# Three edits in one kernel: a fused bias-and-maximum pass, an earlier signal, and a fetch order

## What is computed

```python
# sparse attention, for a block of 128 queries (528 keys: 16 meta tokens and 512 tokens)
_, sel = lax.top_k(score, topk)                       # 128 keys for each query
logits = jnp.einsum('bqhc,bqkc->bqhk', qf, kv_sel).astype(jnp.float32) * scale
logits = jnp.where(valid[:, :, None, :], logits, -1e30)
p = jax.nn.softmax(logits, axis=-1)
...
# experts: every token goes to 2 of 32
hid = jax.nn.silu(xe @ w1[e]) * (xe @ w3[e])          # w1, w3: 1024 x 512
return hid @ w2[e]                                    # w2: 512 x 1024
```

## Time and profile before

| | before |
|---|---|
| median of 3 runs | 2671.62 us (2663.79 to 2676.19) |
| the profiled execution | 2671.74 us, its span 2669.9 us |
| busy: TensorE, VectorE, ScalarE, GpSimd | 91%, 61%, 33%, 33% of the span |
| sparse attention | about 300 to 514 us |
| experts | about 645 to 1123 us |

### The profile page before, as it was taken

How to read it: one execution, slowest core, us unless ns; L and a number is a source line. 1 busy time by engine, 2 the same in 40 slices (tenths; PEclk the granted TensorE clock), 3 DMA queues, 4 the chain that set the end, 5 groups by cost and what they waited for, 6 DMA issues and landing times.

```text
span 2669.9 us, 32591 instructions
## 1 busy us (share of the span) xinstructions
PE 2418.1 (91%) x12845; PEld 1821.7 (68%) x12845; DVE 1623.2 (61%) x3273; ACT 868.5 (33%) x1619; POOL 882.5 (33%) x714
## 2 busy tenths in 40 slices
PE   9999888997888878789899967699999999999999
PEld 7756555675545444377675556588888888888887
DVE  5357567443100100054536999789988888898887
ACT  3135333431000000043422248633343333333333
POOL 0013211001110010000001169586666666566660
PEclk9999878997999998979999978899999999999999
DMA  4344110245999999641123006799999999999994
GB/s 186 124 174 181 52 44 32 98 189 232 411 426 426 426 426 425 265 171 67 41 86 150 25 20 241 249 409 398 367 399 392 388 388 391 358 394 397 407 394 144
DMA packets 137549, 693.66 MB, mean 260 GB/s; under 512 B 18364, under 2 KB 36836, under 8 KB 103600
## 3 DMA queue, kind: packets, MB, share of 16 engines
q1 hardware_dynamic: 76656, 479.68, 45.1%
q0 software_dynamic: 60736, 211.85, 20.4%
HBM read 659.52 MB, written 38.81 MB: 262 GB/s over the span
## 4 chain that ended last, share of the span: by engine, by line
PE 69%; DVE 17%; DMA 8%; ACT 4%; issue 2%; SPq 0%; DVEq 0%; ACTq 0%; POOLq 0%
PE psum L3422 13%; PE psum L3388 11%; DMA arena<-w 7%; PE psum L1706 6%; PE psum L2752 4%; PE psum L2217 4%; PE psum L466 4%; PE psum L982 4%; PE psum L1713 3%; DVE arena L3569 3%; DVE rounded L3519 2%; PE psum L3394 2%; PE psum L3392 2%; PE psum L1285 2%; PE psum L1300 2%
## 5 line engine op out<-in xcount | busy, mean ns | idle before, releaser
L3422 PEld LDWEIGHTS psum<-rounded,rounded 128*128 128x128 f32 x2880 | 429.7, 188 | 25.8 <-ACT rounded L3455 10.1
L3422 PE MATMUL psum<-rounded,rounded 128*128 128x320 f32 x2880 | 443.9, 310 | 0.3
L3388 PE MATMUL psum<-rounded,rounded 128*128 128x512 f32 x1536 | 399.3, 396 | 6.7 <-DVE rounded L3533 6.7
L3335 POOL DMA_INDIRECT arena<-u_rows,arena x192 | 295.6, 1540 | 152.4 <-DVE arena L3574 48.8
L3335 POOL DMA_INDIRECT arena<-v_rows,arena x192 | 286.1, 1490 | 168.8 <-DVE arena L3580 73.3
L3388 PEld LDWEIGHTS psum<-rounded,rounded 128*128 128x128 f32 x1536 | 284.3, 189 | 82.3 <-issue 19.6
L1706 PE MATMUL psum<-arena 128*64 128x256 f32 x2048 | 256.6, 414 | 62.5 <-issue 47.9
L3519 DVE TENSOR_TENSOR rounded<-arena,rounded 128x1024 fp32r<-128x1024 f32 x248 | 302.3, 1219 | 8.1 <-ACT rounded L3455 8.1
L1706 PEld LDWEIGHTS psum<-arena 128*64 128x64 f32 x2048 | 179.1, 150 | 151.7 <-issue 103.5
L1817 DVE COPY arena<-psum 128x256 f32<-128x256 f32 x32 | 13.6, 424 | 419.9 <-PE psum L1758 419.9
L3455 ACT ACTIVATE rounded<-arena 128x1024 fp32r<-128x1024 f32 x248 | 247.7, 1045 | 0.1
(11 more groups left out here) (473 smaller groups left out, 3762.1 us busy)
## 6 DMA issues: line engine op xcount, KB each, us to landing
arena<-w SPq DMA_DIRECT2D x96, 2048.0 KB, 27.8
arena<-uv SPq DMA_DIRECT2D x124, 1024.0 KB
arena<-wada SPq DMA_DIRECT2D x12, 2048.0 KB
arena<-gd SPq DMA_DIRECT2D x30, 640.0 KB
arena<-wp SPq DMA_DIRECT2D x8, 2048.0 KB
gd<-arena SPq DMA_DIRECT2D x11, 1024.0 KB, 11.3
arena<-win SPq DMA_DIRECT2D x4, 2048.0 KB
arena<-wq SPq DMA_DIRECT2D x4, 2048.0 KB
```

What stands on the lines that cost most here:

```text
L3335: po.indirect_dma_start(out=ROWS_OF[i % len(ROWS_OF)], out_offset=None, in_=src, in_offset=bass.IndirectOffsetOnAxis(ap=column.bitcast(U32 ...
L3388: ins = pe.matmul(PS[:, 2 * n + half, :], gg[:, z, 128 * n:128 * n + 128], v[:, y, 512 * half:512 * half + 512], x == 0 and i == 0, x == 1 ...
L3422: ins = pe.matmul(PS[:, 7, 0:DT], w[:, y, k, :], hv[:, z, :], k == 0 and i == 0, k == 7 and i == 2)
```

## The change

Three edits. (1) In the sparse attention one VectorE instruction forms `-(logits + bias)`, writes it to `PB`, and gives its row minimum, which is the negated row maximum of the sum, to `MX`; the separate maximum is gone, and ScalarE takes exp(-PB + MX). The signal `max` is gone with it, ScalarE waits for `logits`. (2) The up products of w1 and of w3 each wait for their own matrix only and signal apart, as `w1` and `h`; the SiLU waits for `w1`. (3) SP issues the fetches in the order w1(e), w3(e), w2(e - 1), in which TensorE uses them, and the fetch to the place of a w1 waits for the signal `w1`.

```diff
@@ sparse_ac
-                    ac.wait_ge(*D.dv["max", n, g, h])
-                    ac.activation(PB[:, h, 0:nk], PB[:, h, 0:nk], ACT.Exp, bias=MX[:, h:h + 1],
+                    ac.wait_ge(*D.dv["logits", n, g, h])
+                    ac.activation(PB[:, h, 0:nk], PB[:, h, 0:nk], ACT.Exp, bias=MX[:, h:h + 1], scale=-1.0,
                                   accum_out=SM[:, h:h + 1]).then_inc(*D.ac("exp", n, g, h))
@@ sparse_dv
-                    dv.tensor_tensor(view(n, PB[:, h, :]), PS[:, b:b + np_, 0:w], view(n, SCM[n % 2]), ALU.add).then_inc(
-                        *D.dv("logits", n, g, h))
-                    dv.wait_ge(*D.dv["logits", n, g, h])
-                    dv.tensor_reduce(MX[:, h:h + 1], PB[:, h, 0:nk], AX, ALU.max, negate=True).then_inc(*D.dv("max", n, g, h))
+                    dv.tensor_tensor_reduce(view(n, PB[:, h, :]), PS[:, b:b + np_, 0:w], view(n, SCM[n % 2]), -1.0, 3.0e38,
+                                            ALU.add, ALU.min, MX[:, h:h + 1]).then_inc(*D.dv("logits", n, g, h))
@@ experts
+    def up_matmul(pe, wt, xt, x0, b):
+        for k in range(8):
+            for half in range(2):
+                ins = pe.matmul(PS[64 * half:64 * half + CAP, b, 0:256], xt[:, k, x0:x0 + CAP],
+                                wt[:, k, 256 * half:256 * half + 256], k == 0, k == 7)
+        return ins
...
+    IN_TURN = [0, 1] + [i for e in range(1, 32) for i in (3 * e, 3 * e + 1, 3 * e - 1)] + [95]
+
     def experts_sp(sp):
-        for i in range(9, 96):
-            sp.wait_ge(*M.pe["y" if i % 3 == 2 else "h", i // 3 - 3])
+        for i in IN_TURN:
+            if i < 9:
+                continue
+            sp.wait_ge(*M.pe[("w1", "h", "y")[i % 3], i // 3 - 3])
             fetch_expert(sp, i)
@@ experts_pe
-                for m in range(2):
-                    pe.wait_ge(*ring[PLACES[(3 * up + m) % 9][0]]["expert", 3 * up + m])
                 for half in range(2):
                     pe.wait_ge(*M.dv["xt", up // 2, half])
                 if up > 1:
                     pe.wait_ge(*M.dv["h", up - 2])
                 x = up % 2
-                up_matmuls(pe, place(3 * up, 8), place(3 * up + 1, 8), XET[(up // 2) % 2], CAP * x, 2 * x).then_inc(*M.pe("h", up))
+                for m, name in enumerate(("w1", "h")):
+                    pe.wait_ge(*ring[PLACES[(3 * up + m) % 9][0]]["expert", 3 * up + m])
+                    up_matmul(pe, place(3 * up + m, 8), XET[(up // 2) % 2], CAP * x, 2 * x + m).then_inc(*M.pe(name, up))
@@ experts_ac
-                ac.wait_ge(*M.pe["h", e + 1])
+                ac.wait_ge(*M.pe["w1", e + 1])
                 ac.activation(HS[x], PS[:, 2 * x, 0:256], ACT.Silu).then_inc(*M.ac("h", e + 1))
```

More of the change, by code:

```diff
@@ L1700, in place @@
         return at3(PLACES[i % 9][1], kk, 4096 // kk)
-    def up_matmuls(pe, w1, w3, xt, x0, b):
[L1703 to L1708, removed]
+    def up_matmul(pe, wt, xt, x0, b):
[4 more added lines that the diff above has]
+        return ins
+    def up_matmuls(pe, w1, w3, xt, x0, b):
+        up_matmul(pe, w1, xt, x0, b)
+        return up_matmul(pe, w3, xt, x0, b + 1)
     def down_matmuls(pe, w2, ht, b):
```

## The result

| | before | changed |
|---|---|---|
| median of the runs | 2672.06 us (6 runs) | 2649.47 us (6 runs) |
| ratio, 95% interval | | 0.9902 [0.9887, 0.9917] |
| profiled execution | 2671.74 us | 2645.66 us |

The account below looks back on a forecast made before the run. The expert stage was taken as bound by DMA, sparse attention as shared by TensorE and VectorE. Fused pass 5.0, front 6.5 and back 7.5 made 19.0 us off 2671.62: 2652.7 us, range 2646 to 2667.

Parts of the forecast that it names:

- Part 2, the front: Start of the expert stage: earlier signals and fetches in order of use fill the DMA hole; 6.5 us, bounds 3.6 and 7.3.
- rival (d): Fetches issued earlier enter a queue already full; front and back give 0 to 3 us; 2665 us, 10%.
- the earlier first fetch alone: Lower bound at the expert stage's front: the tenth matrix's fetch goes out 3.6 us sooner, gaining 3.6 us.
- Part 3, the back: End of the expert stage: less TensorE work stands behind the last w3's landing; 7.5 us, bounds 4 and 8.2.
- rival (a): The expert stage's tail gives nothing or half, as DMAs are unordered across engines and w2(30) could land late; 2659 us, 15%.
- rival (c): Expert stage: many short waits hold TensorE's clock at its lower level; with four tenths of its work there, 2709 us, 5%.
- Part 1, the fused pass: Sparse attention: removing 32 row maxima from VectorE shortens TensorE's waits; 5.0 us, bounds 2 us lost and 7.6 gained.
- the term for TensorE's clock: Sparse attention: shorter waits might keep the clock up at n = 1 and n = 2; 2.6 us, upper bound only.
- rival (b): Sparse attention: the fused pass streams at half rate, as a Trainium skill page suggests for two non-bf16 SBUF sources; 2659.7 us, 8%.
- no second wait: Sparse attention, block n = 0: TensorE has no second wait for the change to remove, so 0.2 us are lost.
- L1175 gone: Sign that the fused pass works as forecast: source line L1175 no longer appears in the profile.
- waits at L1007 under 1 us: Sign that the forecast holds: TensorE's waits at source line L1007 fall under 1 us.

Follow-up runs that it names:

- the part kernels: The kernel before with the fused pass for some query blocks only: n = 0 alone 0.9991, n = 1 and 2 only 0.9997, n = 3 only 0.9993.
- the first four experiments: In the order told, against the kernel before: fused pass alone 0.9961, signals and fetch order alone 0.9956, order alone 0.9985, signals alone 0.9990.

## Why the prediction was off

**What bounds the kernel**: right. The expert stage stayed full of DMA, only its ends moved; what follows was shifted whole.

**Part 2, the front**: 6.5 us taken. The last landing came 1093.0 - 633.7 = 459.3 us after the stage's start, against 466.3: 7.0. Right, which rules out rival (d), but its lower bound wasn't: "the earlier first fetch alone" is worth 0 and not 3.6, as the run with the signals alone showed. Order is what brings the front, 4.6 us, and on top of it the signals give the rest.

**Part 3, the back**: 7.5 us taken; 11.4 from the last landing to the end before, 1096.8 - 1093.0 = 3.8 after: 7.6. Right too, which rules out rival (a). Apart, order gave 4.9 and signals 3.6.

**The clock of the expert stage**, rival (c): the other way. It rose from 0.93 to 0.99 with waits for `w` of at most 2.0 us in place of 3.58 us in one piece. It brought nothing, as said, since DMA is the bound: the stage gained only its ends. The Trainium skill (TensorE: Matmul & The Clock Gate, HAM oscillation) tells of a kernel whose TensorE falls back to the lower clock in each wait for a DMA between short bursts of products. The trace agrees: behind 3.58 us of waiting a whole up product took 8.81 us, and with the waits cut up a half product takes 3.67 and the mean clock is up.

**Part 1, the fused pass: the step that failed.** The step is the term for TensorE's clock: put at nothing in the sum, allowed for only as a bonus of 2.6 us in the upper bound. 5.0 us were taken for the part, 7.6 as the upper bound; 10.4 were measured for it alone (7 to 14), and giving VectorE its time back cost 12 (6 to 18).
Its price was right (705 ns for 702, and 83 for the read-out), so rival (b) is out. The page behind that rival speaks of two sources in SBUF; here one is in PSUM, so the page's sentence doesn't bear on this instruction.
The waits were nearly right in sum. From the first logits product of a group to the next gate product, the eight groups took 30.6 us before and 22.9 after, by block (us):

| block | forecast | shorter by | of it the lower level | the waits |
|---|---|---|---|---|
| n = 0 | -0.2 | 1.0 | 0.3 | 0.6 |
| n = 1 | 1.7 | 1.9 | 0.2 | 1.7 |
| n = 2 | 2.4 | 2.6 | 0.8 | 1.8 |
| n = 3 | 1.1 | 2.2 | 0.8 | 1.4 |
| sum | 5.0 | 7.7 | 2.1 | 5.6 |

The sum's closeness hides two errors of reading in opposite directions: for n = 0 I wrote "no second wait", as the timeline prints none, but each group has one of 0.33 us inside it; and n = 2 gave less than taken.
The clock was the larger term. I allowed the gate products behind the two longest waits 1.3 us each and took none of it. All 13 had lost 13.1 us together, and the change gave back 5.6 (8.2 in the profile of the pass alone), besides the 2.1 in the logits products: 7.7 us of the stage's 15.1. With the 5.6 of the waits that leaves 1.8 us, which I didn't trace. The sentence "the other 20 or so maxima lie beside gate products and are worth nothing" didn't hold as a statement on the whole stage; through the clock the change was worth more than the waits. The runs with spare products show that this isn't the waits over again: VectorE's work unchanged, 10.8 us of gate products gone.
With 10 to 12 us for this part the sum would have been 24 to 26. The profile before shows what the clock had taken from the gate products (13.1 us), not how much of it would come back: fusion in two blocks brought none. And the half microsecond by which the stated range was missed is itself within the noise, whereas 19.0 lies outside the 22 to 30 of the result.

**What stays open**: why the clock follows the pattern as it does. Full fusion gives back 5.6 to 8.2 us of gate products against the profile before, fusion in n = 1 and 2 takes 1.0 away, and the part kernels can't be told from adding up or not. Kernels with the same sparse stage differ by 3 us in it. The rise and fall depend on more than the wait just ahead.

**Right or wrong signs**: of those that I had named, L1175 gone, the pass within 0.1 us, no hole, TensorE under 4 us behind the traffic, and landing waits under 2 us (2.0 the longest) came out; "waits at L1007 under 1 us" didn't (1.01 and 2.08): after the fusion VectorE's search for the next block's top keys still stands ahead of the bias. And one sign of being wrong did appear: the waits in front of down products grew from 16.5 to 27 us. It cost nothing, as the stage is bound by the DMA that they wait for.

**The best version** tried is the changed kernel with spare products, 0.9884 and 0.9877 beside 0.9902 and 0.9904.

## What to carry to other kernels

Where a stage of TensorE alternates waits and products, add up what its undisturbed kind of product takes and compare with what all of them took: the difference is what the clock takes there, and the most that an edit of the waits can win back through it. In this case full fusion won back about half, fusion in two blocks nothing. A group of the timeline may hide waits inside, and a slow group may hold no wait but the lower clock: measure from the first instruction of one group to the first of the next, and compare the mean time of one product. In this stage, full of DMA, only the hole at the start and the chain behind the last landing were to be had: fetch in the order of use, and put as little as possible behind the last landing.

## What was not expected of the hardware

Most of the scatter of the whole time goes with the granted clock: in 35 runs of the kernel before, beside the first four experiments, the mean clock ran from 0.938 (2681.9 us of span) to 0.946 (2662.2 us), with a correlation of -0.87 between clock and span. And useless work made the kernel faster: products whose result is thrown away took the sparse stage from 191.5 to 181.8 us before, and from 176.4 to 170.6 us in the changed kernel.
